# The order of VectorE's and ScalarE's pieces in four turns of attention, TensorE's order kept

## The reference

```python
q, kv_c, kv_s, kv_w, gates = nsa_project(a, w_in, q_gain)
# compressed branch: 64 compressed keys of each sequence
logits = q @ rmsnorm(kc) + bias;  p = masked_softmax(logits);  o_c = p @ vc;  imp = p.sum(heads of the group)
# selected branch: 16 of 32 blocks of 64 rows, chosen by imp, all other blocks masked out
score = where(forced, 1e4, imp_sel);  _, idx = top_k(score, n_top)
rows = pool[page_table ...];  p = masked_softmax(q @ rmsnorm(rows.k) + bias);  o_s = p @ rows.v
# window branch: the last 512 rows
p = masked_softmax(q @ rmsnorm(window.k) + bias);  o_w = p @ window.v
o = gates[0] * o_c + gates[1] * o_s + gates[2] * o_w
```

## Time and profile before

| what | value |
|---|---|
| median of three runs | 1217.02 us (1216.89 to 1227.86) |
| profiled execution, its own time | 1213.46 us |
| its span in the trace | 1211.7 us |
| TensorE matmuls busy | 1169.2 us, 96% |
| VectorE, ScalarE, GpSimd busy | 39%, 23%, 18% |
| chain that ended last | TensorE 90%, VectorE 5%, issue 2%, ScalarE 2% |
| mean granted TensorE clock | 0.996 |

### The profile page before, as it was taken

The page is one execution under the profiler, slowest core; times in us unless marked ns, Lnnn a source line. Parts: engine busy times, 40 slices in busy tenths (PEclk is TensorE's granted clock), DMA queues, the critical chain, the costliest instruction groups (busy, mean ns, idle before and its releaser), DMA issues.

```text
span 1211.7 us, 36160 instructions
## 1 busy us (share of the span) xinstructions
PE 1169.2 (96%) x14724; PEld 970.7 (80%) x14724; DVE 477.0 (39%) x1391; ACT 277.2 (23%) x707; POOL 221.4 (18%) x376
## 2 busy tenths in 40 slices
PE   9999999999999999999788789999999999999998
PEld 7888887999999987874355467787797887977977
DVE  3111116677775333104688872441121221212324
ACT  1000013101010122325887751301011011010131
POOL 5134332011340000413355520100000000000000
PEclk9999999999999999999999999999999999999999
DMA  9999899998442474653698869599999999999821
GB/s 328 338 320 294 299 334 280 212 374 294 139 168 96 183 291 161 178 106 105 211 315 265 274 233 402 168 382 384 376 343 376 368 370 396 341 352 381 317 99 40
DMA packets 123096, 329.97 MB, mean 272 GB/s; under 512 B 17880, under 2 KB 56873, under 8 KB 121268
## 3 DMA queue, kind: packets, MB, share of 16 engines
q1 hardware_dynamic: 96772, 259.88, 58.8%
q0 software_dynamic: 16656, 59.30, 16.5%
q10 hardware_dynamic: 9504, 8.48, 2.3%
HBM read 319.16 MB, written 15.70 MB: 276 GB/s over the span
## 4 chain that ended last, share of the span: by engine, by line
PE 90%; DVE 5%; issue 2%; ACT 2%; DMA 0%; DVEq 0%; SPq 0%; ACTq 0%
PE bank L2096 19%; PE bank L2795 16%; PE bank L2217 12%; PE pbank L2806 6%; PE bank L2253 6%; PE bank L2154 5%; PE pbank L2795 4%; PE bank L2806 3%; PE bank L2342 2%; PE bank L2747 1%; PE bank L2431 1%; PE bank L2544 1%; PE bank L2550 1%; PE bank L2505 1%; PE pbank L2747 1%
## 5 line engine op out<-in xcount | busy, mean ns | idle before, releaser
L2795 PE MATMUL bank<-X,gring 128*64 128x96 f32 x4608 | 195.4, 246 | 3.7 <-issue 3.6
L2795 PEld LDWEIGHTS bank<-X,gring 128*64 128x64 f32 x4608 | 191.8, 137 | 7.8 <-issue 7.8
L2096 PE MATMUL bank<-aT,gring 128*128 128x288 f32 x704 | 175.2, 407 | 0.0
L2096 PEld LDWEIGHTS bank<-aT,gring 128*128 128x128 f32 x704 | 133.0, 190 | 37.1 <-issue 0.9
L2806 PE MATMUL pbank<-Q,X 128*32 128x256 f32 x1152 | 77.7, 379 | 0.0
L2217 PE MATMUL bank<-aT,gring 128*128 128x144 f32 x528 | 72.3, 286 | 1.1 <-issue 1.0
L640 POOL DMA_DIRECT2D Q<-in_cache_cmp x96 | 51.8, 540 | 113.0 <-PE bank L2154 78.5
L2022 DVE TENSOR_TENSOR X<-X,bank 128x96 f32<-128x96 f32 x72 | 18.4, 256 | 131.3 <-ACT X L1344 130.8
L2015 DVE TENSOR_TENSOR hT<-hT,bank 128x288 f32<-128x288 f32 x48 | 18.9, 449 | 129.4 <-PE bank L2747 129.4
L2217 PEld LDWEIGHTS bank<-aT,gring 128*128 128x128 f32 x528 | 67.7, 190 | 1.4 <-issue 1.1
L2096 PE MATMUL bank<-Q,gring 128*128 128x288 f32 x256 | 63.3, 408 | 0.1
(11 more groups left out here) (409 smaller groups left out, 1794.4 us busy)
## 6 DMA issues: line engine op xcount, KB each, us to landing
gring<-in_moe SPq DMA_DIRECT2D x176, 512.0 KB, 6.5
Q<-in_moe SPq DMA_DIRECT2D x72, 512.0 KB, 7.1
gring<-in_dense_gu SPq DMA_DIRECT2D x44, 512.0 KB, 12.8
gring<-in_conv_in SPq DMA_DIRECT2D x24, 512.0 KB, 10.7
Q<-in_cache_cmp POOLq DMA_DIRECT2D x96, 128.0 KB, 5.5
Q<-in_cache_cmp SPq DMA_DIRECT2D x96, 128.0 KB, 5.0
gring<-in_dense_down SPq DMA_DIRECT2D x16, 704.0 KB, 5.3
Q<-in_cache_cmp ACTq DMA_DIRECT2D x64, 128.0 KB, 4.8
```

The costliest lines, as they stand in the source:

```text
L2096: ins = pe.matmul(bank(label, k)[:, 0:T], tile[:, 128 * i:128 * i + 128], rhs[:, i, :], start=i == 0, stop=i == C - 1)
L2795: ins = pe.matmul(m_bank(i, M_GU + f)[64 * w:64 * w + 64, CAP * u:CAP * u + CAP], gslot(("m", 0), 2 * f + u)[:, o:o + 64], ae[:, c, :], st ...
```

## The change

Pieces change places in the lists of ScalarE and VectorE. No instruction is added or taken away, and the lists of TensorE, GpSimd and SyncE stay as they are. The first two hunks are ScalarE's, the last two VectorE's.

```diff
                 if p == 0:
                     token_values(2)
-                key_squares(p, 6)
                 key_scale(p, 2)
                 if p == 0:
                     folded_values()
+                key_squares(p, 6)
                 transposed(p, 0)
...
                 exps(1, S[:, 1536:2048], smt[:, 3:4], sexp_ready)
                 if p < 3:
+                    key_squares(p + 1, 2)
                     key_scale(p + 1, 0)
                 transposed(p, 5)
                 if p < 3:
-                    key_squares(p + 1, 2)
                     key_squares(p + 1, 3)
                 transposed(p, 2)
                 if p < 3:
+                    window_exps(p + 1)
                     importance(p + 1)
                 transposed(p, 4)
-                if p < 3:
-                    window_exps(p + 1)
                 prompt_exps(2 * p + 1, 0)
                 transposed(p, 3)
```

```diff
                 prompt_scores(2 * p, 1)
+                window_factor(p)
                 if p:
                     selected_values(p - 1, 0)
                     selected_values(p - 1, 1)
-                window_factor(p)
-                if p:
                     prompt_transposed(2 * p - 1, 1)
...
                 prompt_scores(2 * p + 1, 0)
                 if p:
-                    prompt_out(2 * p - 1)
                     selected_values(p - 1, 2)
                 selected_scores(p, 3)
                 soft(1, mxt[:, 3:4], smax_ready)
                 if p:
                     selected_values(p - 1, 3)
+                    prompt_out(2 * p - 1)
                 prompt_scores(2 * p + 1, 1)
                 prompt_scale(2 * p)
                 prompt_transposed(2 * p, 0)
                 if p < 3:
                     window_scores(p + 1)
                 prompt_transposed(2 * p, 1)
-                if p < 3:
-                    blocks_chosen(p + 1)
                 prompt_out(2 * p)
                 if p:
                     sample_out(p - 1)
+                if p < 3:
+                    blocks_chosen(p + 1)
             selected_factor(3)
```

## The result

| what | before | after |
|---|---|---|
| median (21 runs of each, taken side by side) | 1217.67 us (1212.56 to 1227.86) | 1226.06 us (1221.58 to 1230.89) |
| ratio, 95% interval | | 1.0059 (1.0045 to 1.0072) |
| profiled execution, its own time | 1213.46 us | 1224.11 us |
| its span | 1211.7 us | 1222.0 us |

The account below looks back on a forecast made before the run. TensorE was taken to bound the kernel, with all to win or lose in its stands in the four turns. Turns 0 to 3 at -0.5, 2.7, 2.05 and 2.35 gave +6.6 on 1217.0: 1223.6 us, range 1215.5 to 1230.

Parts of the forecast that it names:

- The choice and GpSimd beside VectorE: Start of turns 1 to 3: moved `blocks_chosen` and GpSimd's later masked table make VectorE 0.55, 1.4, 1.4 us late.
- The page DMAs: GpSimd's tile loads behind the later masked table: key tile lands late for ScalarE, 1.8, 0.3, 0.6 us in turns 1 to 3.
- `prompt_out`: VectorE's `prompt_out(2p - 1)` behind `selected_values(p - 1, 3)`: leaves an idle pocket, costs 0.35 us in each of turns 1 to 3.
- Turn 0: ScalarE's `key_scale(p, 2)` ahead of `key_squares(p, 6)`: removes a TensorE stand of 0.68 us in turn 0, gain 0.5 us.
- The window's scale and the rest: `key_squares(p + 1, 2)` ahead of `key_scale(p + 1, 0)`, and the window and drain pieces that trade places: nothing.
- The rival of the clock: TensorE drops to half clock after grown stands at L2487 and transposes 6, up to four falls of 1.3 us: 1227.6; chance 0.15.
- Covers hold: VectorE is not held by GpSimd's pieces and the tiles land in time: +2.0, 1219.0 us; chance 0.22.
- faster: ScalarE's earlier scale in turn 0 removes 0.68 us of standing and the clock stays up: -1.8, 1215.2 us; chance 0.10.
- Tiles late in every turn: DMAs behind the masked table land 2.9 us past the spare time each turn, clock falls too: 1232 and more; chance 0.08.

Follow-up runs that it names:

- the third experiment: Changed kernel with `selected_factor` computed ahead of the choice of blocks instead of behind it: 1230.46 us, 1.0106 to the kernel before.
- TensorE kept busy: Changed kernel with the first `selected_values(p - 1, t)` of a turn computed twice into the same bank: 1224.33 us, 1.0063 to the kernel before.
- key tile ahead: GpSimd issues ("sk", p, 3, 1) ahead of ("sv", p - 1, 2, 1): on the changed kernel 1222.22 us, 1.0029; with the choice moved alone 1223.06 us, 1.0033.

## Why the prediction was right, step by step

Sign, size and the main step held: 7.2 us by the ratio for 6.6, and the choice moved from under its cover is shown to carry the loss, by that move alone (1.0058) and by its reversal (1.0009). That the size came so close is in part luck: the sum has no term for the clock, which in the profiled execution took 3.6 us, and in its place counts a late tile at 2.7 us, of which 0.2 could be seen there. By the steps:

*The choice and GpSimd beside VectorE.* Forecast 0.55, 1.4, 1.4 us; measured at the stand 0.23, 1.2, 1.2. The place of the hold was wrong in one point: I let both L1867 and L1852 be held, and only the first was. So the 0.15 and more at L1852 fell away (0.79 us in turn 1, 0.75 in turn 2); that it can be held in its turn, the third experiment shows.

The Trainium skill, SBUF — State Buffer, SBUF: two separate sides, calls the shared pair of ports an exclusive lock for a whole instruction. The traces agree: a one-column product took 0.84 us beside pieces of 1.03 us and 0.16 away from them, and the large addition, when it was the one to meet them, 1.49 us for 0.75. The product with an input from PSUM took 0.69 us both times.

*The page DMAs.* Forecast 1.8, 0.3, 0.6 us. The tile's DMAs came 2.3 us later in the turn, not 3.6: the masked table stretched by 0.45 us, not 0.9, and GpSimd had less idle time between its tiles (0.88 us before this one for 1.36, and none before the one ahead for 0.16, so that the prediction's 1.36 us before each tile was misread). In turn 1 the price is 1.8 us if the clock stays up (TensorE kept busy) and 0.1 to 0.2 if it falls first or in the same stretch (both profiles of the changed kernel); in turn 2 it is 0.7 us with TensorE kept busy and 0 in the other. By the ratios the late tile is worth 0.0025 to 0.0035, 3 to 4 us in all (0.0059 against 0.0029, 0.0058 against 0.0033, 0.0063 against 0.0028). In the profiled turns 1 to 3 I find 1 to 3 us of it (135.9, 136.2 and 135.3 us against 134.5 and 133.3), 1.0 to 1.5 of them in turn 1; but those three have a fall in turn 1 and the two with the tile ahead have none, so the profiles alone can't tell tile from fall. By the ratios the forecast's 2.7 is about right; where the microseconds lie is not settled.

*`prompt_out`.* Forecast 0.35 a turn; measured 0.29 in turn 1 and 0.33 in turns 2 and 3, and it is what is left when the choice is put back (0.89 for 0.60). Right.

*Turn 0.* Forecast -0.5. The stand before keys 2 is gone, as forecast: the row at 580.01 has no idle time, had 0.68. In the second profile turn 0 is 0.4 us shorter. In the first it is 0.4 longer, because half the clock lasted from 588.7 to 595.6 us there, where before it was 590.5 to 593.9.

*The window's scale and the rest.* Forecast nothing. With the choice put back, all of this and `prompt_out` are still in, and the ratio is 1.0009: nothing that can be told.

*The rival of the clock.* It came true in turns 2 and 3 at the stands that I named, with 1.2 us a fall. In turn 1 the fall was not at transposes 6, where I had it, but at L2485, behind 1.72 us; the argument that the stands of 1.5 us did not bring it about doesn't hold either: in the second execution it came behind 1.46 us. I gave the rival 0.15 and priced it on top of everything, at 1227.6. It does not add up like that: a fall in front of a late tile hides it, and when the fall is kept away the tile shows. That is why forecast and rival were both close, and neither was the whole. "Covers hold" and "faster" are out, since the covers were gone in every turn. "Tiles late in every turn", at 2.9 us each, is out: turn 2 shows 0 to 0.7.

What stays open: what each fall is worth over many runs. Keeping TensorE busy changed no ratio (0.0059 to 0.0063 without the key tile ahead, 0.0029 to 0.0028 with it), though it raised the mean clock by 0.0029 and 0.0026, over 3 us of full clock. Without the key tile ahead the tile that then shows (1.8 and 0.7 us) accounts for it. With it nothing that I found does; but the two ratios have 0.002 on either side, and a gain of 2 us would be lost in them.

## What to carry to other kernels

A piece that is done while its engine would wait anyway is free only there; before moving it, look at how much idle time the place it goes to has, and at what waits for its result on the third engine: here 2.2 us of VectorE's time cost 1.2 in two turns of three directly, and about as much again through a GpSimd list in which DMAs stand behind the work that it released. Where compute and DMA issues share one strict list, put the transfer with the least spare time ahead first. And two delays in the same stretch are not always added: work out which one is last, and what is last when it is gone.

## What was not expected of the hardware

Half the clock after a stand is not a fixed consequence of the stand. In one execution of the changed kernel it came behind stands of 1.72, 2.67 and 2.68 us, in another of the same program not behind the 1.72 and the 2.68 us of turns 1 and 2, but behind one of 1.46 us and the one of turn 3 (2.67). In the four turns every fall lasted 3.4 or 6.8 us. Where it could be read between two matmuls, one of 3.4 us cost 1.0 to 1.6 us and one of 6.8 us 2.5 (key tile ahead, turn 3). The hold of VectorE by GpSimd is not in proportion to the instruction's size: the one-column product paid 0.6 us, the large addition 0.75.
